# Two lent SBUF places of each layer of the second block hold first halves of split weights, in place of weights as they land

## Chip, cores and metric

The kernel runs on one core of a Trainium2 chip. The metric is the device time of one execution in microseconds (us). On this core TensorE (PE) multiplies, ScalarE (ACT) and VectorE (DVE) do elementwise work, GpSimd (POOL) helps them, and SyncE (SP) issues the transfers from HBM.

## What is computed

Two transformer blocks run one after the other on 256 tokens of width 2048, all in fp32. The first block is done when the change begins to matter. The second block has two layers, and each does this:

```python
mod = silu(c) @ w_mod[l] + b_mod[l]                      # shift, scale, gate
h = rmsnorm(x, norm_gain[l]) * (1 + scale) + shift
q_a, k_a, v_a, g_a, q_i, k_i, w_i, q_b, k_b, v_b, g_b = split(h @ w_in[l])
att = sparse_attention(norm(q_a), norm(k_a), v_a, q_i, k_i, w_i, ...)   # top 64 keys of each row
y_a = att * silu(g_a)
ret = retention(rotary(q_b), rotary(k_b) * 128 ** -0.5, v_b)
y_b = head_groupnorm(ret) * silu(g_b)
x = x + gate * (concat(y_a, y_b) @ w_out[l])
```

## The kernel before

**Weights.** All weights are read once from HBM, 512 KB at a time. Such a piece of 128 partitions x 1024 fp32 numbers is called a chunk, and the chunks are numbered in the order of their use. The first layer of the second block (layer 0) has chunks 617 to 815, layer 1 has 816 to 998. The fp32 product is formed from rounded halves (type fp32r), so each chunk of a product goes through four steps, each on an engine of its own:

- `send(j)` on SP: the transfer into a *raw place*;
- `split(j)` on ACT (its copy is recorded as L1370): the chunk, rounded, goes into a *place for first halves*, w;
- `split(j)` on DVE (recorded as L1821, SCALAR_TENSOR_TENSOR): what the first half lacks is written over the raw place, which is then called ring_r or AR_r;
- `gemm_part(j)` on PE (L150): 16 products of 128x256, eight with either half, some 1.9 us for most chunks.

Chunks of `w_mod` need only a raw place and one DVE instruction (`macc<-ring,sm,macc`). Both places of a chunk are given back when PE has finished `gemm_part(j)` (or DVE the `w_mod` chunk).

**Places.** `ring` has R1 = 7 raw places, `w1` has R2 = 5 places for first halves (printed w). While a stretch of the working buffer AR isn't used, it is lent as further places by `lend(name, base, word, kind, until, after)`: kind "raw" adds a raw place, kind "w1" a place for first halves. A lent place for first halves is printed AR_r when ACT writes it. In the second block QB and KB name the space of the rotated q and k of the retention; QI is the space of the indexer's q. `lend_start` runs at the start of a layer; `lend_qi` adds two raw places once the indexer's products are done.

**Order.** One list, `steps`, is written by a planner when the program is built, and each engine executes its own part of it, strictly in that order. The planner has no costs: it goes through the chunks, and before each `gemm` it puts a split for every chunk that has been sent and for which a place for first halves is left (`look_ahead`), and after each `gemm` a send for every raw place that has come free (`send_all`). The jobs of attention and retention (copies out of PSUM, top-k, softmax) are `phase` steps between them. So the number of places of a kind decides how far ahead of its product a chunk is sent or split, and thus between which other work its instructions stand.

Of the kernel before, what the change touches and what calls it, by code (L numbers as in the profile page):

```python
# [209 lines left out]
def program(nc, t, out, ctx):  # L210
    def sb(name, shape, dt=F32):
        return ctx.enter_context(nc.sbuf_tensor(name, shape, dt))
# [18 lines left out]
    w1 = sb("w1", [128, R2, CH], F32R)  # L231
# [156 lines left out]
    def add(w, c0, n, kt, orient, x, kind, at, need=None, dup=False, fresh=False, k0=0, quiet=False):  # L388
        b = dict(quiet=quiet, w=w, c0=c0, n=n, kt=kt, orient=orient, x=x, kind=kind, at=at, need=need, dup=dup, fresh=fresh, k0=k0)
        blocks.append(b)  # L390
        per = min(kt, CH // n)
        for k in range(0, kt, per):
            chunks.append(("w", b, k, min(per, kt - k)))
        return b
# [44 lines left out]
    def inline(kind, *at):  # L439
        job = Job(kind, *at)  # L440
        for seg in range(len(PAUSES.get(kind, ())) + 1):
            phase(job, seg)

    def enqueue(q, jobs, seg=0):

        q.append([[(j, s, (PAUSES[j.kind] + (0,))[s]) for j in jobs
                   for s in range(seg, len(PAUSES[j.kind]) + (j is jobs[-1]))], 0])
# [77 lines left out]
    def lend(name, base, word, kind, until, after):  # L525

        last = max(i for i, c in enumerate(chunks) if c[1] is until)
        plain, rounded = base
        if kind == "raw":
            s = Slot((plain[:, word:word + CH], rounded[:, word:word + CH]), in_lent[len(loans)], last)  # L530
            raw_free.append((s, after))
        else:
            s = Slot(rounded[:, word:word + CH], None, last)
            w1_free.append((s, after))
        loans[name] = s
        send_all()
# [7 lines left out]
    def norm(meanwhile=()):  # L544
        for line in xlines:
            while line[0]:
                phase(*line[0].pop(0)[:2])
        xlines.clear()
        job = Job("norm", norm_now[0])
        for seg in range(10):  # L550
            phase(job, seg)
            if 2 * seg - 2 in meanwhile:
                ensure(meanwhile[2 * seg - 2])
        norm_now[0] += 1
# [99 lines left out]
    def launch(*jobs):  # L654
        return lambda: [enqueue(queue, [j]) for j in jobs]
# [11 lines left out]
    def lend_ar(name, word, kind, until, *after):  # L667
        lend(name, (AR, ARR), word, kind, until, list(after))
# [58 lines left out]
    def layer2(L):  # L727
        WIN, h = t["w_in_2"][L], f"h{2 + L}"

        def start():  # L730
            inline("rstd", 2 + L)
            if L == 0:
                inline("decay")
                free_stages.append((NSTG, []))
            norm()
            inline("gate", L)
            if L == 0:
                enqueue(short, [Job("scalex")])

        def lend_start():  # L740
            before = (gemm, (b_out if L else b_down)["end"])
            if L == 0:
                lend_ar("W0", 11008, "raw", b_qi[0], before)
                lend_ar("V0", 8960, "raw", b_vb[0], before)
                lend_ar("V1", 9984, "w1", b_vb[0], before)
            lend_ar(f"QB0{L}", 4864, "raw", b_rot[L][0], before)
            lend_ar(f"QB1{L}", 5888, "w1", b_rot[L][1], before)
            lend_ar(f"KB0{L}", 6912, "raw", b_rot[L][2], before)
            lend_ar(f"KB1{L}", 7936, "raw", b_rot[L][3], before)

        def lend_qi():
            over = (idx_pe, ("p7", L))
            lend_ar(f"QI0{L}", 2816, "raw", b_rot[L][1], over)
            lend_ar(f"QI1{L}", 3840, "raw", b_rot[L][3], over)

        def lend_sparse():
            over = (sp_pe, ("pv", L, 3))
            lend_ar(f"W{L + 1}", 11008, "raw", b_last if L else b_qi[1], over)
            if L == 1:
                lend_ar("B0", 13312, "raw", b_last, over)  # L760
                lend_ar("B1", 14336, "raw", b_last, over)
                lend_ar("B2", 15360, "w1", b_last, over)

        def lend_retain():
            over = (ret_pe, ("sv", L, 3))
            lend_ar(f"V{2 * L + 2}", 8960, "raw", b_last if L else b_vb[1], over)
            lend_ar(f"V{2 * L + 3}", 9984, "w1", b_last if L else b_vb[1], over)

        add(WIN, 2304, 512, KT, "CM", h, "qi", (L, 0), [lend_start, start], fresh=True)
        add(WIN, 3328, 128, KT, "CM", h, "ki", (L,), dup=True)  # L770
        add(WIN, 3392, 16, KT, "TM", h, "wi", (L,))
        b_qi.append(add(WIN, 2816, 512, KT, "CM", h, "qi", (L, 1)))
        add(WIN, 1024, 128, KT, "CM", h, "kn", (L,), [launch(Job("indexer", L))])
        add(WIN, 0, 512, KT, "CM", h, "qn", (L, 0))
        add(WIN, 512, 512, KT, "CM", h, "qn", (L, 1))
        add(WIN, 1152, 128, KT, "TM", h, "va", (L,))
        for blk in range(2):
            b = add(WIN, 3408 + 512 * blk, 512, KT, "CM", h, "rot", (L, "q", blk),
                [launch(Job("retain", L, 0), Job("retain", L, 1))] if blk
                else [lend_qi, lambda: enqueue(queue, [Job("sparse", L, hp) for hp in range(4)])])  # L780
            b_rot[L][blk] = b
            b_rot[L][2 + blk] = add(WIN, 4432 + 512 * blk, 512, KT, "CM", h, "rot", (L, "k", blk))
            b = add(WIN, 5456 + 512 * blk, 512, KT, "TM", h, "vb", (L, blk))
            if blk == 0:
                b_vb.append(b)
        for blk in range(2):
            b = add(WIN, 1280 + 512 * blk, 512, KT, "CM", h, "glu", (L, "a", blk),
                    [lend_sparse] if blk else [launch(Job("retain", L, 2), Job("retain", L, 3))])
            b_g.setdefault(L, b)
        for blk in range(2):  # L790
            add(WIN, 6480 + 512 * blk, 512, KT, "CM", h, "glu", (L, "b", blk), None if blk else [lend_retain])
        for blk in range(4):
            b = add(t["w_out_2"][L], 512 * blk, 512, KT, "TM", f"o{L}", "oevac", (L, blk),
                    [lambda: inline("ahead")] if blk == 3 and L == 0 else None, fresh=blk == 0,
                    quiet=blk == 3 and L == 0)
        return b

    marks, b_g, b_qi, b_rot, b_vb = {}, {}, [], [{}, {}], []
# [1765 lines left out]
```

How the kernel before makes its waits and increments, by code:

```python
    def hold(e, J, *names):  # L841
        for name in names:
            for s, ev in J.hold[name]:
                e.wait_ge(*s.after(*ev))
# [45 lines left out]
    def given_back(e, *names):  # L891
        for name in names:
            for j in loans[name].users[-1:]:
                s, ev = over(j)
                e.wait_ge(*s.after(*ev))
# [48 lines left out]
        def send(j):  # L945
            kind, b, k, m = chunks[j]
            n, landed = b["n"], slot[j].landed
            dst = slot[j].at[0][:, 0:m * n].rearrange("p (k n) -> p k n", n=n)
            k += b["k0"]
            src = b["w"][128 * k:128 * (k + m), :].rearrange("(k p) n -> p k n", p=128)
            c0 = b["c0"]
            for s, ev in held[j]:
                e.wait_ge(*s.after(*ev))
            if b["dup"]:
                h = n // 2
                e.dma_start(dst[:, :, 0:h], src[:, :, c0:c0 + h]).then_inc(*landed.step("half", j))
                e.dma_start(dst[:, :, h:n], src[:, :, c0:c0 + h]).then_inc(*landed.step("w", j))
            else:
                e.dma_start(dst, src[:, :, c0:c0 + n]).then_inc(*landed.step("w", j))
# [1 line left out]
        def final(J, seg):  # L961
            e.wait_ge(*normed(1))
            e.wait_ge(*bias_act.after("e11"))
            e.wait_ge(*rope2_dve.after("sin"))
            e.wait_ge(*rope2_act.after("cos"))
            e.dma_start(GB, t["final_norm"].partition_broadcast(128)).then_inc(*in_final.step("row"))
# [1 line left out]
        def decay_mask(J, seg):  # L968
            e.wait_ge(*bias_act.after("e11"))
            e.wait_ge(*rope2_dve.after("sin"))
```

## Time and profile before

| | |
|---|---|
| runs | 2089.18, 2092.43, 2105.43 us; median 2092.43 |
| profiled execution | 2096.29 us |
| its span, first to last instruction | 2094.5 us |
| mean granted TensorE clock | 0.942 |
| layer 0's stretch in which the plans differ | 1278 to 1512 us |
| layer 1's stretch in which the plans differ | 1693 to 1913 us |
| HBM read | 532.55 MB, 255 GB/s over the span |

PE has the largest busy share of the engines. In a row of the profile, L150 is the matmul line, L1370 and L1821 are the lines of the helpers through which most ACT and DVE work is recorded, so one goes by the names of the tiles. A time in brackets is idle time of the engine just ahead of the instruction, with the releaser that ended it.

### The profile page before, as it was taken

What the parts mean: (1) busy time and instruction counts of PE and PEld (TensorE: products, weight loads), DVE (VectorE), ACT (ScalarE), POOL (GpSimd) and SP (SyncE); (2) the same over time, 40 slices, a digit from 0 to 9 for tenths busy, and PEclk for the clock granted to TensorE, in tenths of its full rate; (3) what the DMA queues carried; (4) which work ended last, traced back from release to release, by engine and by line L of the source; (5) the groups of instructions that cost most, each with busy time, mean ns of one, the idle gap of its engine ahead of it and who ended that gap; (6) DMA issues with size and microseconds to landing.
All of it is one profiled execution on the core that took longest, in us unless ns stands there. A gap on an engine that the chain in (4) does not pass through costs nothing. (4 is left out here: it accounts for less than half of the span.)

```text
span 2094.5 us, 34021 instructions
## 1 busy us (share of the span) xinstructions
PE 1921.8 (92%) x13292; PEld 1788.7 (85%) x13292; DVE 1711.1 (82%) x2198; ACT 1240.4 (59%) x1921; POOL 270.4 (13%) x182
## 2 busy tenths in 40 slices
PE   5998899899999997999899987999989879999798
PEld 5787889899998897989889976998878669988797
DVE  6777777875998898988898986789879876887787
ACT  5456644645566765556666658446666574566664
POOL 0000040031010012221100100132101002221020
PEclk8998899899999998999999998899999988999999
DMA  7785565865999777689889976868689867686885
GB/s 233 236 284 181 191 191 182 293 201 183 353 354 357 238 255 240 227 297 297 296 293 334 317 263 195 268 187 267 223 280 316 307 201 245 203 272 198 282 309 203
DMA packets 270764, 536.88 MB, mean 256 GB/s; under 512 B 31880, under 2 KB 40973, under 8 KB 269581
## 3 DMA queue, kind: packets, MB, share of 16 engines
q1 hardware_dynamic: 270317, 532.62, 75.9%
q8 instruction: 105, 1.72, 0.3%
q10 hardware_dynamic: 288, 2.10, 0.3%
q14 instruction: 54, 0.44, 0.1%
HBM read 532.55 MB, written 2.10 MB: 255 GB/s over the span
## 5 line engine op out<-in xcount | busy, mean ns | idle before, releaser
L150 PE MATMUL ps<-hh_r,w 128*128 128x256 f32 x3384 | 866.8, 295 | 43.6 <-DVE ring_r L1821 23.0
L150 PEld LDWEIGHTS ps<-hh_r,w 128*128 128x128 f32 x3384 | 674.2, 199 | 57.5 <-DVE ring_r L1821 27.7
L150 PE MATMUL ps<-hlo,ring_r 128*128 128x256 f32 x2816 | 707.8, 290 | 0.0
L1821 DVE SCALAR_TENSOR_TENSOR ring_r<-ring,w 128x1024 fp32r<-128x1024 f32 x449 | 555.7, 1254 | 165.0 <-ACT w L1370 162.3
L1370 ACT ACTIVATE w<-ring 128x1024 fp32r<-128x1024 f32 x449 | 465.2, 1052 | 209.8 <-DMA ring<-in_w_in 94.0
L150 PEld LDWEIGHTS ps<-hlo,ring_r 128*128 128x128 f32 x2816 | 561.4, 199 | 1.0 <-issue 0.7
L150 PE MATMUL ps<-hlo,AR_r 128*128 128x256 f32 x1104 | 268.0, 283 | 0.0
L1821 DVE SCALAR_TENSOR_TENSOR AR_r<-AR,w 128x1024 fp32r<-128x1024 f32 x172 | 214.5, 1262 | 46.0 <-ACT w L1370 45.1
L150 PE MATMUL ps<-w,AR_r 128*128 128x512 f32 x584 | 233.7, 400 | 8.7 <-DVE AR_r L1821 7.9
L1370 ACT ACTIVATE w<-AR 128x1024 fp32r<-128x1024 f32 x172 | 178.9, 1056 | 66.6 <-DMA AR<-in_w_in 23.4
L150 PEld LDWEIGHTS ps<-hlo,AR_r 128*128 128x128 f32 x1104 | 213.0, 193 | 0.3 <-issue 0.2
L150 PE MATMUL ps<-ring_r,AR_r 128*128 128x512 f32 x504 | 200.3, 397 | 0.0
L150 PE MATMUL ps<-AR 128*128 128x64 f32 (+5 forms) x1340 | 181.7, 297 | 18.7 <-DVE AR L1817 12.7
L150 PEld LDWEIGHTS ps<-AR 128*128 128x128 f32 (+1 forms) x1340 | 165.9, 197 | 28.3 <-issue 18.3
L150 PE MATMUL ps<-hh_r,AR_r 128*128 128x256 f32 x664 | 162.9, 284 | 3.1 <-DVE ring_r L1821 3.1
L150 PE MATMUL ps<-AR_r 128*128 128x512 f32 (+1 forms) x480 | 161.5, 377 | 3.1 <-DVE ring_r L1821 3.1
L1821 DVE SCALAR_TENSOR_TENSOR macc<-ring,sm,macc 128x1024 f32<-128x1024 f32 x121 | 163.4, 1350 | 0.0
L150 PEld LDWEIGHTS ps<-w,AR_r 128*128 128x128 f32 x584 | 111.4, 191 | 35.0 <-DVE AR_r L1821 5.9
L1821 DVE SCALAR_TENSOR_TENSOR ring_r<-ring,AR_r 128x1024 fp32r<-128x1024 f32 x91 | 118.6, 1308 | 20.2 <-ACT AR_r L1370 19.7
L150 PE MATMUL ps<-w,hh_r 128*128 128x512 f32 (+2 forms) x368 | 130.2, 363 | 5.4 <-DVE ring_r L1821 3.3
L150 PEld LDWEIGHTS ps<-hh_r,AR_r 128*128 128x128 f32 x664 | 127.1, 191 | 5.9 <-DVE ring_r L1821 4.9
L2407 POOL TENSOR_TENSOR AR<-AR 128x1024 int32<-128x1024 int32 (+2 forms) x25 | 55.2, 2209 | 549.8 <-DVE AR L1821 439.1
(204 smaller groups left out, 2765.5 us busy)
## 6 DMA issues: line engine op xcount, KB each, us to landing
ring<-in_w_in SPq DMA_DIRECT2D x285, 512.0 KB, 5.2
ring<-in_w_mod SPq DMA_DIRECT2D x131, 512.0 KB, 5.5
ring<-in_w_up SPq DMA_DIRECT2D x115, 512.0 KB, 5.5
AR<-in_w_in SPq DMA_DIRECT2D x83, 512.0 KB, 5.7
ring<-in_w_out SPq DMA_DIRECT2D x63, 512.0 KB, 6.5
ring<-in_w_down SPq DMA_DIRECT2D x63, 512.0 KB, 5.9
AR<-in_w_up SPq DMA_DIRECT2D x61, 512.0 KB, 5.5
AR<-in_w_mod SPq DMA_DIRECT2D x48, 512.0 KB, 6.1
```

Source lines behind the costliest of these rows:

```text
L150: return e.matmul(o, l, x, start=start, stop=stop, skip_group_check=True)
L1370: return e.activation(o, i, ACT.Copy, scale=scale)
L1821: return e.scalar_tensor_tensor(o, a, s, b, op0, op1)
L2407: return e.tensor_tensor(o, a, b, op)
```

## The change

In each layer, the two places KB0 and KB1 are lent for first halves and no longer for weights as they land. Chunks are sent, split and multiplied in the same order as before, by the same instructions; the places they use differ, and the point in each engine's program at which a send or a split stands.

```diff
             lend_ar(f"QB0{L}", 4864, "raw", b_rot[L][0], before)
             lend_ar(f"QB1{L}", 5888, "w1", b_rot[L][1], before)
-            lend_ar(f"KB0{L}", 6912, "raw", b_rot[L][2], before)
-            lend_ar(f"KB1{L}", 7936, "raw", b_rot[L][3], before)
+            lend_ar(f"KB0{L}", 6912, "w1", b_rot[L][2], before)
+            lend_ar(f"KB1{L}", 7936, "w1", b_rot[L][3], before)
```

Worked out from the planner, in layer 0 (layer 1 is alike): where there were 11 raw places and 7 for first halves, there are now 9 and 9, until `lend_qi` adds two raw places ahead of chunk 662. When PE begins a `gemm` in chunks 640 to 661, the chunks sent beyond it were 10 and are now 8; those split, with its own, were 7 or 8 and are now up to 9, which is all that has been sent. From chunk 664 on, 9 are sent ahead where there were 11, and 7 to 8 split as before. The plans are the same again from about chunk 715 and, in layer 1, about 914.

First place: ACT in layer 0, around the copies of the first half of q_a out of PSUM (L1376 and L1370 with VT). The names in_ring and in_lent are the signals of landing. Before:

```order
L1370 ACTIVATE w<-ring 128x1024 [waits gemm_done,in_ring5]
L1370 ACTIVATE AR_r<-ring 128x1024 [waits gemm_done,in_ring6]
L1370 ACTIVATE AR_r<-ring 128x1024 [waits gemm_done,in_ring0]
L1376 ACTIVATE stg<-ps 128x512 [waits gemm_done,idx_pool]
L1370 ACTIVATE AR<-ps,VT 128x512
L1376 ACTIVATE stg<-ps 128x512 [waits gemm_done,idx_pool]
L1370 ACTIVATE AR<-ps,VT 128x512
L1370 ACTIVATE w<-ring 128x1024 [waits gemm_done,in_ring1]
```

The same place after the change:

```order
L1370 ACTIVATE AR_r<-ring 128x1024 [waits gemm_done,in_ring4]
L1370 ACTIVATE AR_r<-ring 128x1024 [waits gemm_done,in_ring5]
L1370 ACTIVATE w<-ring 128x1024 [waits gemm_done,in_ring6]
L1376 ACTIVATE stg<-ps 128x512 [waits gemm_done,idx_pool]
L1370 ACTIVATE AR<-ps,VT 128x512
L1376 ACTIVATE stg<-ps 128x512 [waits gemm_done,idx_pool]
L1370 ACTIVATE AR<-ps,VT 128x512
L1370 ACTIVATE w<-ring 128x1024 [waits gemm_done,in_ring0]
```

The split just ahead of the four copies was that of chunk 657, which SP sent behind the product of chunk 646; it is now that of chunk 659, sent behind the product of chunk 650, the last but one ahead of the copies.

Second place: DVE in layer 0, around the first product of the retention (`stg<-ps,AR`, L1813), whose masked scores PE takes next. Before:

```order
L1821 SCALAR_TENSOR_TENSOR macc<-ring,sm,macc 128x1024 [waits mod_dve,in_ring5]
L1821 SCALAR_TENSOR_TENSOR ring_r<-ring,w 128x1024 [waits w1_done]
L1994 RECIPROCAL sm<-sm 128x4 [waits sp_act]
L1821 SCALAR_TENSOR_TENSOR ring_r<-ring,AR_r 128x1024 [waits w1_done]
L1813 TENSOR_TENSOR stg<-ps,AR 128x512 [waits ret_pe,in_decay,rot_pool,qn_dve]
L1813 TENSOR_TENSOR stg<-ps,AR 128x256
```

The same place after the change:

```order
L1821 SCALAR_TENSOR_TENSOR macc<-ring,sm,macc 128x1024 [waits mod_dve,in_ring1]
L1821 SCALAR_TENSOR_TENSOR AR_r<-AR,AR_r 128x1024 [waits w1_done]
L1994 RECIPROCAL sm<-sm 128x4 [waits sp_act]
L1821 SCALAR_TENSOR_TENSOR AR_r<-AR,AR_r 128x1024 [waits w1_done]
L1821 SCALAR_TENSOR_TENSOR ring_r<-ring,w 128x1024 [waits w1_done]
L1813 TENSOR_TENSOR stg<-ps,AR 128x512 [waits ret_pe,in_decay,rot_pool,qn_dve]
L1813 TENSOR_TENSOR stg<-ps,AR 128x256
```

One more split, which waits for ACT's, stands between the reciprocal and the product.

Third place: ACT in layer 0, ahead of the copies of the second half of the retention's q (`stg<-ps 64x512`). Before:

```order
L1376 ACT_TABLE_LOAD
L1376 ACTIVATE sm<-sm 128x4 [waits ret_act]
L1370 ACTIVATE w<-ring 128x1024 [waits gemm_done,in_ring6]
L1370 ACTIVATE stg<-ps 64x512 [waits gemm_done,rot_pool]
L1370 ACTIVATE stg<-ps 64x512
```

The same place after the change:

```order
L1376 ACT_TABLE_LOAD
L1376 ACTIVATE sm<-sm 128x4 [waits ret_act]
L1370 ACTIVATE AR_r<-ring 128x1024 [waits gemm_done,in_ring2]
L1370 ACTIVATE w<-ring 128x1024 [waits gemm_done,in_ring3]
L1370 ACTIVATE stg<-ps 64x512 [waits gemm_done,rot_pool]
L1370 ACTIVATE stg<-ps 64x512
```

Two splits, of chunks 710 and 711, stand ahead of the copies in place of one, of chunk 710; chunk 711 is now sent behind the product of chunk 702, two products ahead of the copies.

## Rows read from the trace of the kernel before

**Rows 1.** The page, busy time of each engine over the span

```profile
PE 1921.8 (92%) x13292; PEld 1788.7 (85%) x13292; DVE 1711.1 (82%) x2198; ACT 1240.4 (59%) x1921; POOL 270.4 (13%) x182
```

**Rows 2.** The page, groups: splits (busy, mean ns of one, idle before, releaser)

```profile
L1821 DVE SCALAR_TENSOR_TENSOR ring_r<-ring,w 128x1024 fp32r<-128x1024 f32 x449 | 555.7, 1254 | 165.0 <-ACT w L1370 162.3
L1370 ACT ACTIVATE w<-ring 128x1024 fp32r<-128x1024 f32 x449 | 465.2, 1052 | 209.8 <-DMA ring<-in_w_in 94.0
```

**Rows 3.** Windows: length; busy PE, PEld, DVE, ACT, POOL; clock, DMA share, GB/s

```profile
1303.00:1345.00 42.00, 40.59 (x288) 40.59 (x289) 32.81 (x35) 21.26 (x26) 0.00 (x0) 0.80 0.83 269
...
1426.00:1465.00 39.00, 36.07 (x231) 32.29 (x230) 36.06 (x37) 22.47 (x37) 15.59 (x8) 1.00 0.81 265
...
1512.00:1560.00 48.00, 43.68 (x290) 39.15 (x290) 36.74 (x41) 27.49 (x67) 3.91 (x2) 1.00 0.85 277
...
1888.00:1893.00 5.00, 5.00 (x25) 5.00 (x25) 3.31 (x4) 2.08 (x9) 0.00 (x0) 0.50 0.00 0
```

**Rows 4.** PE's waits, 1304 to 1426 (total us, times, longest)

```profile
PE ps L150 <- DVE ring_r L1821: 7.8, 1, 7.8
PE ps L150 <- DVE AR_r L1821: 0.3, 1, 0.3
```

**Rows 5.** PE's waits, 1426 to 1512

```profile
PE ps L150 <- DVE stg L1813: 2.1, 1, 2.1
PE ps L150 <- issue: 1.8, 1, 1.8
...
PE ps L150 <- ACT stg L1370: 1.1, 1, 1.1
```

**Rows 6.** PE's waits in layer 1, 1718 to 1840, then 1840 to 1915

```profile
PE ps L150 <- ACT AR L1370: 1.5, 1, 1.5
...
PE ps L150 <- DVE stg L1813: 4.6, 1, 4.6
```

**Rows 7.** ACT's longest wait, 1345 to 1396, then 1512 to 1560

```profile
ACT w L1370 <- PE ps L150: 13.9, 10, 2.3
...
ACT w L1370 <- DMA ring<-in_w_in: 14.6, 9, 3.0
```

**Rows 8.** Issues, 1345 to 1396, then 1404 to 1426 (median us to landing last)

```profile
ring<-in_w_in SPq DMA_DIRECT2D x14, 512.0 KB, 4.0
...
ring<-in_w_in SPq DMA_DIRECT2D x5, 512.0 KB, 4.8
```

**Rows 9.** Timeline, SP, ACT and PE, first half of q_a (start, us)

```profile
1373.11 0.37 SPq L959 DMA_DIRECT2D AR<-in_w_in  x1
...
1375.04 0.60 ACT L1376 ACTIVATE stg<-ps 128x512 f32<-128x512 f32 x1 [0.81 <-PE ps L150]
...
1376.69 1.84 PE L150 MATMUL ps<-cst,stg 128*128 128x1 f32 x16
```

**Rows 10.** Timeline, SP, ACT and PE, around the first q_b copies

```profile
1420.92 0.37 SPq L959 DMA_DIRECT2D ring<-in_w_in  x1
...
1423.17 2.42 ACT L1370 ACTIVATE stg<-ps 64x512 f32<-64x512 f32 x4
1425.62 0.87 ACT L1370 ACTIVATE AR<-ps 128x512 f32<-128x512 f32 x2
...
1427.75 1.47 PE L150 MATMUL ps<-AR 128*128 128x256 f32 x8
```

**Rows 11.** Timeline, DVE, the last split and the retention's product behind it

```profile
1473.39 1.23 DVE L1821 SCALAR_TENSOR_TENSOR ring_r<-ring,AR_r 128x1024 fp32r<-128x1024 f32 x1 [2.59 <-ACT AR_r L1370]
1474.54 1.01 DVE L1813 TENSOR_TENSOR stg<-ps,AR 128x512 f32<-128x512 f32 x2
```

**Rows 12.** Timeline, SP, ACT and PE, around the second q_b copies

```profile
1489.06 0.37 SPq L959 DMA_DIRECT2D ring<-in_w_in  x1
...
1492.33 2.42 ACT L1370 ACTIVATE stg<-ps 64x512 f32<-64x512 f32 x4 [1.09 <-PE ps L150]
...
1499.27 0.63 PE L1341 MATMUL ps<-cst,stg 128*128 128x128 f32 x4 [1.32 <-DVE stg L1813]
```

**Rows 13.** Timeline, DVE, one of the splits between steps of top-k

```profile
1387.51 1.23 DVE L1821 SCALAR_TENSOR_TENSOR AR_r<-AR,w 128x1024 fp32r<-128x1024 f32 x1
```

## The prediction

> **What bounds the kernel now.** First the busy shares of the page. PE is busy for 1921.8 of 2094.5 us, DVE for 82% and ACT for 59% [rows 1]; so an ACT or DVE instruction costs time only where it makes PE wait, and one that is late by more than its slack costs the rest in full. The change adds no instruction, no byte and no matmul. All it can do is shift when a chunk is sent and where its splits stand, so I read next how the weights are supplied in the stretches in which the plans differ.
>
> The windows come second [rows 3]. In 1303 to 1345 PE is busy for 40.59 of 42 us at 0.80 clock; in 1426 to 1465 DVE (36.06 of 39) is as full as PE (36.07); in 1512 to 1560, where the lent places are gone and both plans have 7 raw and 5 first-half places, PE still gets 43.68 of 48 us. The reader is to see that DMA isn't full in any of them (0.81 to 0.85). Transfers take 4.0 us from issue to landing, 4.8 in a fuller stretch [rows 8], against 1.9 us of PE for a chunk: eight chunks ahead would be some 15 us, so the number of raw places isn't short in itself.
>
> Third come PE's own waits. In layer 0 up to 1426 they are one of 7.8 us at the layer's start and one of 0.3 us for a weight [rows 4]; then 2.1, 1.8 and 1.1 us, none for a weight [rows 5]. In layer 1 they are 1.5 us behind an ACT copy and 4.6 us behind DVE's retention product [rows 6]. **Weights that are split too late cost PE almost nothing now.** More places for first halves can win little here.
>
> Fourth come ACT's waits. In 1345 to 1396 ACT waits at its splits for PE to free a first-half place (13.9 us in 10 waits, no wait for a transfer); in 1512 to 1560, with 7 and 5 places, it waits for transfers (14.6 us in 9) [rows 7]. With 9 and 9 places the first stretch takes on the second's nature: every chunk sent is split at once, so ACT, which executes in order, stands at a split until that chunk has landed, and the copies out of PSUM behind it are late.
>
> A rule of the Trainium skill speaks against the change. The trace shows the ACT splits of 1345 to 1396 waiting for no transfer [rows 7]. The Trainium skill, "DMA: Bandwidth & Descriptors", section "Rules for kernel authors", says to issue a transfer early and wait for its semaphore late, and the change does the reverse for ACT's splits. The rule names no size; by it the time rises, and by the rows alone the question is what stands behind each split.
>
> **The change, part by part.** Instructions: zero, the same splits of 1.05 us on ACT and 1.25 on DVE [rows 2]. The four places where the order changes for a copy that PE soon needs are these, in layer 0:
>
> *A, first half of q_a.* The split ahead of the copies is now that of chunk 659, sent when PE has done chunk 650: 1373.11 [rows 9], where before this slot sent chunk 661. Landing takes 4.0 [rows 8], the split 1.05 [rows 2]: 1378.2. The copies began at 1375.04 [rows 9], so they start 3.1 us later. PE's sums on them ran at 1376.69 [rows 9], just as the second copy ended, with no slack. Term: +3.1.
>
> *A2, the second half of q_a.* The same order, but both top-k and softmax work stand between and give slack. No row shows how much: bounds 0 and 3.1 (A). I take 0.5, near zero, because PE goes through five chunks without a wait there and needs the sums late.
>
> *B, first half of q_b.* The split of chunk 678 stands at the same step as before, but its chunk is sent at 1420.92 [rows 10] and no longer two products earlier. It lands at 1420.9 + 4.8 = 1425.7 [rows 8], is split at 1426.8, then come the copies of 2.42 and 0.87 [rows 10]: 1430.0. PE's products of attention (ps<-AR) ran at 1427.75 [rows 10]. Term: 1430.0 - 1427.75 = +2.2.
>
> *C, the retention's first product.* DVE waited 2.59 us for an ACT split, split, then started the product at 1474.54 [rows 11], and this product is what PE's wait of 2.1 us ends on [rows 5]. Now one more ACT split stands ahead of the ACT copies and one more between them and the product. Term: 2 x 1.05 - 0.1 overlap = +2.0 at least; a landing on top would make it 2.6. I take 2.0. Every microsecond shows, as PE waits there already.
>
> *D, second half of q_b.* The split of chunk 711 now stands ahead of the copies. It is sent behind chunk 702 at 1489.06 [rows 12], after chunk 710 (0.4 for its issue), lands 4.2 later (between 4.0 and 4.8) [rows 8] and is split by 1494.8. The copies began at 1492.33 [rows 12]: 2.5 late. DVE's rotation and the retention's group norm queue behind them, and PE already waits 1.32 for that at 1499.27 [rows 12]. Term: +2.5.
>
> Layer 0: 3.1 + 0.5 + 2.2 + 2.0 + 2.5 = 10.3. **Layer 1** has the same A, A2 and B. At C only one ACT split is added (1.05, and up to a half more with its landing; I take 1.4), at D PE's slack is some 0.6 larger (1.9). Near its end the place of one chunk (918) comes back with chunk 911's product instead of 909's, when only some 2 to 3 us of slack are left: bounds 0 and one landing of 4.8 [rows 8], I take 1.5, a third, since the DVE queue has slack of its own. Sum: 3.1 + 0.5 + 2.2 + 1.4 + 1.9 + 1.5 = 10.6. Gross: 20.9.
>
> *What is absorbed.* A, A2 and B stop PE for 5.8 us in a layer before a stretch that DVE bounds (36.06 of 39 busy) [rows 3]. There PE has waits that don't grow if it comes late: 2.1 + 1.8 + 1.1 = 5.0 in layer 0 [rows 5], and the 4.6 and a like 1.8 in layer 1 [rows 6]. Bounds: nothing, or 5.0 and 5.8. DVE is nearly full, but part of its work hangs on PE's products, so I take somewhat less than the upper: 4 and 5, together -9.
>
> *What is gained.* Between steps of top-k DVE takes one split in about 3.5 us (one of them at 1387.51) [rows 13], slower than PE's 1.9, and only 0.3 us of PE wait comes of it [rows 4]; with 9 chunks split ahead that wait goes: -0.3 a layer. The 1.5 us of layer 1 [rows 6] come from a copy behind a split that waits for its landing; the order there is changed, and I take -1.4 (bounds -1.5 and 0, and the reverse can't be excluded by the rows). The waits of 7.8 and 4.6 us at the layers' starts end on a split that stands behind the norm in either plan: 0. Together -2.
>
> *Covers.* Two fewer sent ahead: at chunks 640 to 661 there are 8, some 15 us of PE work, against 4.0 to 4.8 of landing plus 1.05 and 1.25 of splits, 7.1 at most. That covers the smaller number of raw places wherever ACT is not held up. If the cover fails, PE waits for weights: see the rivals.
>
> Sum: 20.9 - 9 - 2 = +9.9. The span becomes 2104.4 and the profiled execution 2106.2 (it lies 1.8 above its span). The profiled run was 3.9 above the median, so I carry the difference and not the level: 2092.4 + 9.9 = 2102.3.
>
> The landings come from the trace. By the Trainium skill, "DMA: Bandwidth & Descriptors", section "Anatomy of one DMA", a transfer costs about 2.0 us and its bytes by 436 GB/s, for 512 KB an estimate of 3.2 us, measured there on another issue path. The trace has 4.0 to 4.8. By this figure A, B and D would be smaller by 0.8 to 1.6 each, and the sum by some 6, which still leaves it above zero.
>
> **The rivals.** *Absorbed.* All that A, B, C and D hold up is small against the slack of later work, or PE's waits at C and D merely take another name. For it: DVE and PE are equally full in the middle [rows 3], and each wait is under 3.1. Against it: C and D lie on waits of PE itself [rows 5, 12]. Upper absorption (10.8) with C and D halved (20.9 - 4 - 10.8 - 2) gives +4; with both covered wholly, 0. Time: 2092 to 2096, say 2094.
>
> *Deeper splits win.* A chunk that is split nine ahead is ready however long top-k holds DVE, and fewer transfers are in flight at once. Then the waits of 0.3, 1.5 and a part of 7.8 and 4.6 [rows 4, 6] go. At most 14.2 us hang on weights in these rows; I count the small ones and a fifth of the large: -1.8 - 2.5 = -4, so 2088. Against it: the large ones start with the norm, not with a place.
>
> *Starved.* The raw places are what matters: chunks after the layer's start land later because their place comes back later, while the window 1303 to 1345 has PE at 40.59 of 42 [rows 3], and PE waits once or twice for a landing of 4 to 5 us in each layer. +4 to +8 in place of, or beside, the terms above: 2100.
>
> *Slower by over 1%.* This is the other side of the bound. Its mechanism is PE's clock. After the 4.6 us wait in layer 1 the granted clock was 0.50 (1.2 GHz) for the 5 us from 1888 on [rows 3], which costs 2.5 us. PE's short waits (2.1, 1.8, 1.1) [rows 5] left the window 1426 to 1465 at 1.00. If the new waits at A, B, C and D, alone or joined, become long enough to lower the clock in both layers, each costs some 2.5 more: 8 x 2.5 = 20 over the 20.9 - 9 - 2 gives +30, 2122. It decides once A, B and D are 4 us and more, where I have 2.2 to 3.1.
>
> *The change doesn't do what it says.* The order shows that it does: behind the product of chunk 650 SP sends chunk 661 before and chunk 659 after, and so on through chunks 641 to 659.
>
> **How the numbers follow.** A measurement of this kernel tells about 1%, 21 us, from no change. Chances: the forecast (+5 to +16) 0.42; absorbed (-4 to +5) 0.27; starved (+2 to +20) 0.12; deeper splits win (-4 and below, to -10) 0.11; slower by over 1% 0.08. The predicted time is 2102. The range goes from 2087, which leaves out half of the deeper splits' case, to 2116: the gross 20.9 with C at 2.6 in both layers and little absorbed (20.9 + 1.8 + 1 = 23.7). Outside lie the clock's case and the tails. Faster by over 1%: 0.02; within 1%: 0.90; slower: 0.08.
>
> **What would show it.** In the profile after: between 1345 and 1396 ACT waits for DMA where it waited for PE; PE waits 2 to 3 us at the sums behind the first half of q_a, about 2 at the first attention products, and 3 to 4.5 at the retention's first product; top-k costs no PE wait. Total PE busy time unchanged but for clock. Wrong would be: PE waits named ring_r or AR_r in these stretches (starved), PE's waits summing to what they were (absorbed), or landing times that fall, since fewer transfers are in flight, and take A, B and D with them.

## The result, and the profile after

The kernel after the change takes 2131.22 us (median of 4 runs, 2130.18 to 2133.71), the kernel before 2094.76 us beside it (4 runs). The ratio is 1.0182, 95% interval 1.0146 to 1.0218: slower by some 38 us (the medians differ by 36.5, the two profiled executions by 37.4). The profiled execution took 2133.71 us, its span is 2131.9 us. The forecast was 2102 us with 2116 as the upper end.

Where it went is read from windows that hold the same work in both traces. The first pair runs from the end of chunk 641's product to the end of chunk 717's (columns as in [rows 3]). The kernel before:

```profile
1347.15:1516.61 169.46, 162.27 (x1195) 151.82 (x1195) 143.54 (x226) 101.69 (x184) 45.27 (x30) 0.96 0.72 227
```

The kernel after the change, the same 1195 matmuls, then a window at A, and then the four stretches at half clock (granted clock 0.50, 1.2 GHz) that the kernel before doesn't have, or has shorter. They lie behind A, A2, the second attention product and D, the places that the prediction names and the table below measures:

```profile
1344.85:1533.69 188.84, 170.25 (x1195) 159.18 (x1195) 147.14 (x225) 101.70 (x175) 45.78 (x29) 0.92 0.66 210
1376.00:1381.00 5.00, 2.91 (x18) 2.73 (x17) 3.17 (x10) 4.18 (x7) 2.85 (x2) 0.79 0.76 206
1378.90:1385.80 6.90, 6.90 (x34) 6.90 (x34) 6.63 (x29) 2.40 (x3) 0.24 (x1) 0.51 0.16 45
1402.80:1416.50 13.70, 13.66 (x63) 13.42 (x63) 3.22 (x3) 2.51 (x5) 0.00 (x0) 0.50 0.29 96
1464.30:1467.70 3.40, 3.40 (x11) 2.74 (x11) 3.40 (x3) 1.93 (x3) 3.40 (x3) 0.50 0.42 157
1515.50:1518.90 3.40, 3.40 (x18) 3.40 (x17) 2.74 (x4) 1.79 (x5) 0.00 (x0) 0.50 0.00 0
```

The kernel before, its only two stretches at half clock in this part (A2, and behind the wait at C, where the kernel after the change has 3.4 us too):

```profile
1398.30:1408.50 10.20, 10.20 (x49) 10.11 (x48) 5.59 (x5) 2.42 (x6) 0.00 (x0) 0.50 0.32 100
1476.80:1480.20 3.40, 3.40 (x18) 3.40 (x18) 3.40 (x5) 2.09 (x9) 0.00 (x0) 0.50 0.01 3
```

The reader is to see two parts of the loss. The stretch is 188.84 - 169.46 = 19.4 us longer. PE's idle time grew from 7.2 to 18.6 us, by 11.4; its busy time for the same matmuls grew from 162.3 to 170.3, by 8.0, because the granted clock fell from 0.96 to 0.92, in pieces at 0.50 (1.2 GHz): 30.8 us of them where there were 13.6, and half of the 17.2 more is 8.6. Layer 1 is alike: from the end of chunk 840's product to that of 924's it is 183.83 us before (1762.01 to 1945.84) and 204.46 after (1780.10 to 1984.56), 20.6 longer, PE busy for 174.45 and 181.68. The first block differs by 2.3 us and the rest by less, so the two stretches hold the loss.

PE's waits after the change, 1343 to 1434, answer to [rows 4]:

```profile
PE ps L150 <- ACT AR L1370: 3.8, 2, 2.1
PE ps L150 <- DVE AR L1818: 0.8, 1, 0.8
PE ps L150 <- DVE stg L1818: 0.8, 1, 0.8
```

and those in 1434 to 1530 to [rows 5]:

```profile
PE ps L1341 <- DVE stg L1813: 4.6, 1, 4.6
PE ps L150 <- issue: 4.2, 2, 2.3
PE ps L150 <- DVE stg L1813: 3.8, 1, 3.8
PE ps L150 <- ACT stg L1370: 0.7, 1, 0.7
```

No wait is put down to a split weight (ring_r, AR_r); those with a name are for the layer's other work, and the two without one (issue) stand ahead of products of the attention, the first, of 2.3 us, at B. ACT's waits in 1345 to 1396 answer to the first row of [rows 7]:

```profile
ACT w L1370 <- DMA AR<-in_w_in: 12.2, 4, 6.7
ACT AR_r L1370 <- DMA ring<-in_w_in: 10.9, 8, 3.1
ACT w L1370 <- DMA ring<-in_w_in: 3.8, 4, 1.9
```

ACT waited for PE at its splits before; now it waits for transfers, as forecast. How that reaches PE shows at A, the first half of q_a, in the timeline of SP, ACT and PE (answers to [rows 9]):

```profile
1372.48 0.37 SPq L959 DMA_DIRECT2D ring<-in_w_in  x1
...
1376.12 1.06 ACT L1370 ACTIVATE w<-ring 128x1024 fp32r<-128x1024 f32 x1 [1.88 <-DMA ring<-in_w_in]
1377.08 0.58 ACT L1376 ACTIVATE stg<-ps 128x512 f32<-128x512 f32 x1
...
1378.38 3.04 PE L150 MATMUL ps<-cst,stg 128*128 128x1 f32 x16 [2.09 <-ACT AR L1370]
1381.28 0.56 PE L150 MATMUL ps<-hh_r,w 128*128 128x256 f32 x1
```

Chunk 659 is issued at 1372.48, has landed at 1376.1, is split, and only then come the copies and PE's sums, after 2.09 us of wait. What the forecast didn't have is behind it: the sums take 3.04 us where they took 1.84 [rows 9], and the clock is at half from 1378.9 to 1385.8. The place cost 5.3 us, of which 2.1 are wait.

The table has the loss of each place against the kernel before, from the ends of the same chunks' products in the two profiled executions (layer 0 / layer 1). A row of an experiment is read the same way. How good a single profile is shows in layer 1 of e4_layer0_only, which has the plan of the kernel before: 0.1 us in all places but A2, where it is off by 1.7.

| us | indexer | A | A2 | B | 2nd attention product | C | D |
|---|---|---|---|---|---|---|---|
| forecast | 0 / 0 | 3.1 / 3.1 | 0.5 / 0.5 | 2.2 / 2.2 | less than 0 | 2.0 / 1.4 | 2.5 / 1.9 |
| after | 1.7 / 2.7 | 5.3 / 5.4 | 2.9 / 2.7 | 2.4 / 2.4 | 1.2 / 0.1 | 1.0 / 0.2 | 4.9 / 5.7 |
| e1_kb_none | 0 / 0 | 0 / 0 | 0.7 / 6.2 | 2.2 / 2.6 | -0.5 / -0.1 | 1.5 / -1.1 | 2.5 / 0 |
| e8_lag1 | 0.4 / 1.3 | -0.1 / -0.1 | -0.7 / -0.6 | 0.5 / -0.2 | -1.9 / 1.7 | -0.5 / 1.5 | 3.0 / 0.1 |
| e9_lag1_early | 0.4 / 1.5 | -0.1 / -0.1 | 1.0 / 3.8 | 2.2 / 2.3 | -0.4 / 0.7 | 2.3 / 0.2 | 4.8 / 5.8 |
| e10_lag1_late | 1.6 / 2.6 | 3.8 / 5.2 | -0.7 / 1.1 | 0.4 / -0.2 | -2.0 / 0.8 | -0.2 / 1.2 | 1.3 / 0 |
| e5_filler | 1.5 / 1.9 | 3.9 / 2.5 | -0.4 / -1.9 | 2.1 / 2.5 | -0.4 / 0.1 | 2.6 / -1.0 | 5.2 / 6.4 |
| e6_quiet | 1.3 / 3.4 | -0.1 / -0.1 | -2.3 / -0.4 | 0.3 / -0.2 | 1.4 / 1.0 | 3.9 / 1.7 | 5.3 / 3.5 |

**D** isn't what the forecast made of it. The lines around it, SP, DVE, ACT and PE, after the change (answers to [rows 11, 12]):

```profile
1487.88 2.43 PE L150 MATMUL ps<-AR,stg 128*128 128x128 f32 x11 [3.77 <-DVE stg L1813]
...
1492.98 0.37 SPq L959 DMA_DIRECT2D ring<-in_w_in  x1
...
1498.06 2.52 DVE L1821 SCALAR_TENSOR_TENSOR ring_r<-ring,w 128x1024 fp32r<-128x1024 f32 x2 [4.97 <-ACT w L1370]
1500.50 0.70 DVE L1817 TENSOR_SCALAR sm<-sm 128x4 f32<-128x4 f32 x1
...
1502.98 0.31 ACT L1376 ACTIVATE stg<-stg 128x128 f32<-128x128 f32 x1 [3.66 <-DVE stg L1813]
...
1506.26 1.04 ACT L1370 ACTIVATE AR_r<-ring 128x1024 fp32r<-128x1024 f32 x1
1507.21 1.04 ACT L1370 ACTIVATE w<-ring 128x1024 fp32r<-128x1024 f32 x1
1508.28 2.42 ACT L1370 ACTIVATE stg<-ps 64x512 f32<-64x512 f32 x4
...
1514.83 0.63 PE L1341 MATMUL ps<-cst,stg 128*128 128x128 f32 x4 [4.59 <-DVE stg L1813]
```

PE waits 3.77 us at C. The sends of chunks 707 and 708 stand behind chunk 698's product, which comes after that wait, so SP issues them at 1492.98 only. Both are split at once: DVE stands for 4.97 us at them, and the retention's mean (sm<-sm at 1500.50), the first link of its group norm, is behind both in DVE's queue. ACT waits 3.66 us for the step behind the mean, so its splits of 710 and 711 and the copies behind them come late, though neither split waits for a landing (711's is the one more of this place, 1.0 us). DVE takes the same two splits and the rotation of the copies before the norm's last step, and that step is what PE waits 4.59 us for at 1514.83; 3.4 us at half clock follow. In the kernel before, 707 is sent ahead of that wait and 708 is split behind the mean.

### The profile page after: what moved, and what is told of

Read it like the earlier page. It is cut to its first block and busy times, and to the rows that moved or that the text cites. A ratio compares the mean times of both kernels' runs of the same rounds, so it can differ in the third digit from the quotient of the medians.

```text
span 2131.9 us, 34021 instructions
## 1 busy us (share of the span) xinstructions
PE 1929.6 (91%) x13292; PEld 1793.6 (84%) x13292; DVE 1717.8 (81%) x2198; ACT 1242.0 (58%) x1921; POOL 270.1 (13%) x182
## 5 line engine op out<-in xcount | busy, mean ns | idle before, releaser
L150 PE MATMUL ps<-hh_r,w 128*128 128x256 f32 x3208 | 822.9, 295 | 47.5 <-DVE ring_r L1821 26.3
L150 PE MATMUL ps<-hlo,ring_r 128*128 128x256 f32 x2912 | 731.6, 290 | 0.0
L150 PEld LDWEIGHTS ps<-hh_r,w 128*128 128x128 f32 x3208 | 639.9, 199 | 60.7 <-DVE ring_r L1821 32.3
L1370 ACT ACTIVATE w<-ring 128x1024 fp32r<-128x1024 f32 x444 | 459.2, 1052 | 231.1 <-DMA ring<-in_w_in 142.1
L150 PEld LDWEIGHTS ps<-hlo,ring_r 128*128 128x128 f32 x2912 | 580.2, 199 | 1.0 <-issue 0.7
L150 PE MATMUL ps<-hlo,AR_r 128*128 128x256 f32 x1008 | 244.5, 283 | 0.0
L150 PE MATMUL ps<-hh_r,AR_r 128*128 128x256 f32 x840 | 206.5, 285 | 3.1 <-DVE ring_r L1821 3.1
L1370 ACT ACTIVATE w<-AR 128x1024 fp32r<-128x1024 f32 x155 | 161.4, 1056 | 77.1 <-DMA AR<-in_w_in 42.5
L150 PEld LDWEIGHTS ps<-hlo,AR_r 128*128 128x128 f32 x1008 | 194.2, 193 | 0.3 <-issue 0.2
L1821 DVE SCALAR_TENSOR_TENSOR macc<-ring,sm,macc 128x1024 f32<-128x1024 f32 x128 | 172.6, 1349 | 10.2 <-DMA ring<-in_w_mod 10.2
L1821 DVE SCALAR_TENSOR_TENSOR ring_r<-ring,AR_r 128x1024 fp32r<-128x1024 f32 x110 | 140.2, 1279 | 41.6 <-ACT AR_r L1370 39.9
L150 PEld LDWEIGHTS ps<-hh_r,AR_r 128*128 128x128 f32 x840 | 161.5, 192 | 6.5 <-DVE ring_r L1821 3.8
L1370 ACT ACTIVATE AR_r<-ring 128x1024 fp32r<-128x1024 f32 x110 | 115.6, 1053 | 65.4 <-DMA ring<-in_w_in 44.6
```

The lines of the kernel that those rows point to most:

```text
L150: return e.matmul(o, l, x, start=start, stop=stop, skip_group_check=True)
L1370: return e.activation(o, i, ACT.Copy, scale=scale)
L1821: return e.scalar_tensor_tensor(o, a, s, b, op0, op1)
```

## Experiments

Each was timed beside the kernel before on its chip (15 to 19 runs of it, medians 2092.4 to 2093.5 us).

**e1_kb_none: as few raw places, no more first halves.** Against the kernel after the change (a second line, which skips the names that are lent for nothing, is left out here):

```diff
-            lend_ar(f"KB0{L}", 6912, "w1", b_rot[L][2], before)
-            lend_ar(f"KB1{L}", 7936, "w1", b_rot[L][3], before)
```

> KB0 and KB1 are lent for nothing in both layers: 9 raw places and 7 for first halves, as few raw places as after the change and as few for first halves as before. The split just ahead of the copies of the first half of q_a is of chunk 657, sent behind chunk 648, three products ahead of the copies (after the change 659, one product ahead; before 657, five ahead). Theory 'late copies' (what costs is that ACT stands at a split until a chunk sent just before has landed, and the copies behind it are late): ACT waits at most 1 us for landings there, PE's wait at those sums is gone; the second q_b place keeps part of its wait, since chunk 710 is sent as late as after. 2094 to 2106 us, ratio 1.000 to 1.006. Rival 'too few raw places' (weights are late because they are sent later): all of the loss stays, 2125 to 2135 us.

Measured: 2104.65 us, ratio 1.0070 (1.0044 to 1.0095), +12 us. ACT's waits in 1345 to 1375 (its page numbers the copy L1368):

```profile
ACT w L1368 <- PE ps L150: 9.3, 5, 2.3
ACT AR_r L1368 <- PE ps L150: 3.8, 2, 1.9
...
ACT w L1368 <- DMA ring<-in_w_in: 0.6, 2, 0.3
```

ACT waits for PE again, and A costs nothing in either layer. Two thirds of the loss have gone although two raw places fewer are there than before. B stays at 2.2 and 2.6 us, as it should: its chunk 678 is sent as late as after the change, and is split at the same step. So a late send costs where a split follows it at once, and the deep splitting made every split such a one. In the profile what stays is B (4.8 us in both layers), C and D of layer 0 (4.0) and, in layer 1, 6.2 us at A2, where PE waited 1.3 us for a weight (ring_r) and then ran at half clock; layer 0 lost 0.7 in the same order. The profiled execution took 2111.38 us, 6.7 above the median, so the 6.2 aren't typical, but a small part of this loss is weights that come late.

**e2_kb0_only: one place each.**

```diff
-            lend_ar(f"KB1{L}", 7936, "w1", b_rot[L][3], before)
+            lend_ar(f"KB1{L}", 7936, "raw", b_rot[L][3], before)
```

> Only KB0 goes to first halves, KB1 stays a raw place: 10 raw, 8 for first halves. Last splits ahead of copies: chunk 658 sent three products ahead (q_a), chunk 678 sent three ahead (q_b), and 710 four ahead (second q_b). 'Late copies': landing of some 4 us has passed within three products of 1.9 to 2.9 us, so nearly nothing: 2092 to 2102 us. 'Too few raw places': about half of the loss, 2110 to 2116 us.

Measured: 2103.84 us, ratio 1.0055 (1.0032 to 1.0078), +11 us: above the 2102 of one theory, far below the 2110 of the other. In its profile A and D are within 0.1 us of the kernel before in both layers and B within 0.8; what it loses (7.5 us in all) lies at the layers' starts, 4.2 and 3.4 us, ahead of the places. There a late copy shows again, in ACT's timeline, layer 0:

```profile
1319.64 1.06 ACT L1370 ACTIVATE AR_r<-ring 128x1024 fp32r<-128x1024 f32 x1 [3.42 <-DMA ring<-in_w_in]
1320.60 1.07 ACT L1370 ACTIVATE AR<-ps 128x512 f32<-128x512 f32 x2
```

PE waits 3.5 us for this copy, and 3.3 us for its like in layer 1; the kernel before made it at 1317.42, and PE waited 0 and 1.5 us. It is the same cause at a place that I hadn't listed.

**e3_lag2 and e8_lag1: the places of the change, fresh chunks not split.** In `next_split`, against the kernel after the change (1 in place of 2 for e8_lag1):

```diff
-        return j if w1_free and j < at_send[0] else None
+        late = 2 if j < len(chunks) and chunks[j][1]["x"] in ("h2", "h3") else 0
+        return j if w1_free and j < at_send[0] - late else None
```

> The kernel after the change with 9 raw and 9 first-half places, but in the second block's input projections the planner splits no chunk that is among the last two sent. Sends stand exactly where they stand after the change; only the splits stand later. 'Late copies': PE's waits behind ACT copies go, 2092 to 2102 us. 'Too few raw places': nothing changes, 2128 to 2135 us.

> As e3_lag2, but only the chunk sent last is held back from being split: at q_a the split ahead of the copies is of chunk 658, sent two products ahead (after the change one, in e3_lag2 three). 'Late copies' makes it a matter of degree: landing of 3.7 plus split 1.05 against two products of 1.9 to 2.9 us, so at most 1 us late at A and no half clock; a rest at B and D. 2098 to 2108 us, above e3_lag2 and far below after.

Measured: 2100.29 us, ratio 1.0034 (1.0021 to 1.0046), with two held back; 2095.67 us, 1.0006 (0.9992 to 1.0020), with one. Sends, raw places and first-half places are those of the kernel after the change, and only the splits stand one chunk later. Of the 40.1 us that the change cost in its two stretches, 34 come back (6.0 stay, most in layer 1); another 5.8 us come from between chunks 717 and 816, where both kernels have the same places and only the held-back split is different (e11_lagall_before gains 6.9 us there). So too few raw places can't be what costs the bulk; some 6 us are left to it or to something else. I had expected less of e8_lag1 than of e3_lag2, and it was the other way round; with two held back DVE gets its splits late enough that PE waits for weights (1.2 us in 1343 to 1434, 4.6 us in three waits behind), and A2 costs 4.1 and 5.9 us. ACT's waits of e8_lag1 in 1345 to 1375:

```profile
ACT AR_r L1371 <- DMA ring<-in_w_in: 9.4, 7, 2.5
ACT w L1371 <- DMA AR<-in_w_in: 3.7, 3, 1.7
ACT w L1371 <- DMA ring<-in_w_in: 1.9, 2, 1.6
```

ACT still waits 15.0 us for transfers (15.2 after the change), and A costs nothing. **The waits for landings cost nothing by themselves here; the last one ahead of a copy does,** and with one more product of time it is over before the copy is due.

**e4_layer0_only.**

```diff
-            lend_ar(f"KB0{L}", 6912, "w1", b_rot[L][2], before)
-            lend_ar(f"KB1{L}", 7936, "w1", b_rot[L][3], before)
+            lend_ar(f"KB0{L}", 6912, "raw" if L else "w1", b_rot[L][2], before)
+            lend_ar(f"KB1{L}", 7936, "raw" if L else "w1", b_rot[L][3], before)
```

> The change in layer 0 alone. If the two layers' losses are separate, about half: the trace of after lost some 19 us in chunks 640 to 717 and some 20 in 838 to 920, so 2111 to 2116 us, and layer 1's chunks take the time that they took before. If there were one common cause (where a place lies, a slower chip), the loss would not follow the layer.

Measured: 2110.89 us, ratio 1.0084 (1.0069 to 1.0099), +18 us, half of the whole. Layer 1's A, B, C and D are within 0.1 us of the kernel before, its A2 within 1.7.

**e5_filler: PE kept busy ahead of the q_a sums.** In PE's `qn`, against the kernel after the change:

```diff
                 hold(e, J, "b")
+                for u in range(0 if J.at[1] % 2 else 16):
+                    fp(pb(J, "b")[:, 0:256], hhi[:, 0, 0:128], hhi[:, 0, :])
                 e.wait_ge(*qn_act.after("copy", *J.at))
```

> The kernel after the change, with 16 products of 128x256 that nobody reads, on PE ahead of its wait for the q_a copies, twice in a layer (A and A2); they are overwritten by the sums. In the trace of after PE waits 2.1 us at A in layer 0 and then runs at 1.2 GHz to 1385.7. Theory 'the wait lowers the clock' (half of the loss at A is clock): PE isn't idle there, the clock stays at 2.4 GHz behind A, and 2 to 3 us come back at each A, some less at A2: 2120 to 2127 us. Rival 'the clock falls by itself there' (the sums with one column each): 16 products of 0.12 us are covered by the wait or add to it, 2131 to 2136 us.

Measured: 2126.61 us (2123.18 to 2130.34; a fourth run, of 3078.99 us at a mean clock of 0.551, which I can't explain, is left out), ratio 1.0162 (1.0140 to 1.0185) against the 1.0182 of the change: the intervals overlap, so the total alone decides nothing. The place does, in PE's timeline:

```profile
1378.75 2.08 PE L150 MATMUL ps<-hh_r 128*128 128x256 f32 x16
1380.89 2.18 PE L150 MATMUL ps<-cst,stg 128*128 128x1 f32 x16
```

and in the windows in front of and behind it:

```profile
1378.00:1382.00 4.00, 3.88 (x32) 3.60 (x30) 2.37 (x5) 3.29 (x6) 2.68 (x2) 1.00 0.92 251
1382.00:1388.00 6.00, 5.95 (x38) 5.99 (x39) 5.77 (x24) 1.91 (x2) 0.19 (x1) 0.72 0.16 34
```

The filler takes the wait's place, the sums are back to 2.18 us, and the clock stays at 1.00 until 1382; but it falls behind, to 0.72 over 6 us, which is 3.4 us at half where there were 6.9. A costs 3.9 and 2.5 us where it cost 5.3 and 5.4, A2 -0.4 and -1.9 where it cost 2.9 and 2.7. So at A 1.4 and 2.9 us were clock that the wait had taken (A2's larger gain, 3.3 and 4.6, may hold other clock: the kernel before runs at 1.2 GHz for a while there too). The sizes are rough: the four gains sum to 12 us in this execution, the fastest of the three, while the medians differ by 4.6. Why the clock still falls behind the filled wait stays open.

**e6_quiet: no split ahead of a block's last product.**

```diff
-            if not (b["quiet"] and k0 + m == b["kt"]):
+            if not ((b["quiet"] or b["kind"] in ("qn", "rot")) and k0 + m == b["kt"]):
```

> The kernel after the change, but no split is put ahead of the last product of a block of q_a, q_b or k_b, so the copies of those blocks stand behind the split of one chunk less: at q_a 658, sent two products ahead of the copies, and at the second q_b 708, sent six ahead. Sends are unchanged. 'Late copies': the waits at A, A2, B and D shrink by most of a product's time, 1.9 us, and the half clock behind A goes: 2100 to 2112 us. If the loss lay with weights or raw places: 2128 us and more.

Measured: 2113.44 us, ratio 1.0099 (1.0075 to 1.0124), +20 us where some 38 stood. A, A2 and B are gone, D isn't (5.3 and 3.5), and C is larger (3.9 and 1.7), as I read it because the splits left out ahead of a block's end are made up for there. That refuted my cause for D: chunk 711's split no longer stands ahead of the copies there. The splits of 707 and 708 still stand ahead of the retention's mean, which pointed to the chain shown above.

**e7_qb1_raw: a step the other way, from the kernel before.**

```diff
-            lend_ar(f"QB1{L}", 5888, "w1", b_rot[L][1], before)
+            lend_ar(f"QB1{L}", 5888, "raw", b_rot[L][1], before)
```

> The kernel before, with QB1 too as a raw place in both layers: 12 raw and 6 for first halves, a step in the other direction. Chunks are sent earlier and split one later. 'Late copies': ACT waits for no landing there before either, so nothing to win, and one split less ahead of top-k may cost a wait for weights: 2090 to 2100 us. 'Too few raw places': faster than before, 2075 to 2088 us.

Measured: 2099.58 us, ratio 1.0023 (1.0002 to 1.0045). More raw places don't help. The step also takes a place for first halves, and the profile shows 1.9 us of PE waits for late splits (ring_r) in 1343 to 1434, so this speaks less plainly than e8_lag1.

**e9_lag1_early and e10_lag1_late: e8_lag1 in two parts.** The condition of e8_lag1 with one more term, for e9_lag1_early:

```diff
+        late = 1 if j < len(chunks) and chunks[j][1]["x"] in ("h2", "h3") and chunks[j][1]["kind"] in ("qi", "ki", "wi", "kn", "qn", "va") else 0
```

and with `("rot", "vb", "glu")` for e10_lag1_late.

> The kernel after the change; the chunk sent last is held back from being split only for the blocks from qi to va, so the splits ahead of the indexer's work and of the first q_a copies stand later, and all from the chunks of the first q_b block on stand as after the change. In the traces of before and after the places lose in us: indexer 1.7 and 2.7 (layer 0, layer 1), A 5.3 and 5.4, A2 2.9 and 2.7, B 2.4 and 2.4, second attention product 1.2 and 0.1, C 1.0 and 0.2, D 4.9 and 5.7. If the places are independent, the indexer and A come back, 15 us: 2114 to 2119 us. If each wait only moves work onto the next one (the losses are one chain), less than 8 come back: above 2122.

> The same for the blocks from the first q_b block on alone, which moves the splits at A2 (whose last splits are of q_b chunks), B, C and D. In particular the split of chunk 708 stands behind the retention's mean step on DVE again, where after the change it stood ahead of it and DVE waited 5.0 us for the splits of 707 and 708, which SP had sent only after PE's wait at C. Independent places: 25 us come back, 2103 to 2109 us, A stays with its 5 us in each layer and D goes. One chain: whatever A starts is carried on, 2115 and more.

Measured: 2117.81 us, ratio 1.0115 (1.0081 to 1.0149), and 2112.48 us, 1.0087 (1.0057 to 1.0117). Against 1.0182 they give back 0.67% and 0.95%, 14 and 20 us, together 34 of the 37 that e8_lag1 gives back (1.0182 - 1.0006). Some 3 us of e10_lag1_late's share come from behind chunk 717, as in e8_lag1. The places are nearly independent: without the wait at A, D stays at 4.8 and 5.8; with it, D falls to 1.3 and 0. The first time lies in the range that independence had given (2114 to 2119), the second 3 us above it (2103 to 2109) and below that of one chain (2115). DVE around the mean in e10_lag1_late, where the split of 708 is behind it (its page numbers the lines one higher):

```profile
1485.51 2.46 DVE L1822 SCALAR_TENSOR_TENSOR ring_r<-ring,w 128x1024 fp32r<-128x1024 f32 x2
...
1491.41 1.22 DVE L1822 SCALAR_TENSOR_TENSOR ring_r<-ring,w 128x1024 fp32r<-128x1024 f32 x1 [2.24 <-ACT w L1371]
```

One split and 2.24 us of wait stand in front of the mean where there were two and 4.97, and PE's wait at the transposes fell from 4.6 to 2.6 us.

**e11_lagall_before and e12_lagall_after.** The chunk sent last is never split, in the whole program; e11 with the places of before, e12 with those of after:

```diff
-        return j if w1_free and j < at_send[0] else None
+        late = 1 if at_send[0] < len(chunks) else 0
+        return j if w1_free and j < at_send[0] - late else None
```

> The kernel before, with the chunk sent last never split, in both blocks. If ACT's standing at a split until the landing costs elsewhere too (7 raw and 5 first-half places leave ACT waiting for transfers in much of the program), up to 1% faster, 2075 to 2090 us. If weights come too late by one product more, slower, up to 2105 us. Likeliest: 2085 to 2097 us.

> The same with the places of the kernel after the change. Against e11 it shows what the two places are worth once the split waits for no fresh chunk: 'late copies' says that they are worth about nothing either way, the same as e11 within 6 us; if deeper splits help at all, faster than e11 by 1 to 5 us.

Measured: 2087.27 us, ratio 0.9978 (0.9962 to 0.9994), and 2093.90 us, 0.9999 (0.9981 to 1.0017). The first is the fastest kernel of the study, by some 5 us, small, but its interval lies below 1; in its profile 7 us come from layer 0's part behind chunk 717. With the split rule mended, the two places as first halves take 6.6 us more than as raw places (the expectation allowed 6); the two intervals overlap a little, so this rest is likely but not shown.

## Why the prediction was wrong

**What bounds.** Right for layer 0: PE waited 0.3 us for a weight before, and not at all after. In layer 1 the waits for ring_r are 1.6 us before (1762 to 1946) and 2.7 after (1780 to 1985), near the end, at chunk 918's place. Right too that ACT would wait for landings where it had waited for PE, 27 us in 1345 to 1396.

**A.** The mechanism was right: landing 3.6 us (4.0 taken), PE's wait 2.1 (3.1 taken). The size was not: the place cost 5.3 and 5.4, since 3.2 us of half clock followed. That is the first failed step. I had the clock as a rival, "it decides once A, B and D are 4 us and more", read off one wait of 4.6 us; it took 2.1 us here. The kernel before had shown as much. I wrote that its waits of 2.1, 1.8 and 1.1 us [rows 5] left the window 1426 to 1465 at 1.00, but the one of 2.1 us, at C, ends at 1475.65, behind that window (PE's timeline):

```profile
1475.65 1.86 PE L150 MATMUL ps<-AR,stg 128*128 128x128 f32 x12 [2.14 <-DVE stg L1813]
```

and the window behind it was at 0.68:

```profile
1475.00:1480.00 5.00, 4.35 (x25) 4.38 (x26) 5.00 (x8) 2.34 (x10) 0.00 (x0) 0.68 0.30 106
```

That reading put the clock at nothing in the sum. The wait's length alone doesn't tell, since the 1.8 us left the clock at 1.00. In layer 0 some 8 of the 19.4 us are clock, half of each stretch that is new: 3.4 at A, 1.7 at A2, 1.7 behind the second attention product and 1.7 at D.

**A2.** I took 0.5 between bounds of 0 and 3.1 for want of a row. It is 2.9 and 2.7: 1.66 us of PE wait (the split ahead of the copies waited 1.11 us for its landing) and a longer piece at 0.50, 13.7 us where there were 10.2. The slack that I assumed wasn't there; the upper bound was the place of the same kind, A, and should have been taken.

**B.** 2.2 forecast, 2.4 and 2.4 measured; e1_kb_none and e8_lag1 show it to be chunk 678's landing.

**C.** 2.0 and 1.4 forecast, 1.0 and 0.2 measured.

**D.** 2.5 and 1.9 forecast, 4.9 and 5.7 measured, by another cause: DVE's queue ahead of the retention's mean, and sends held back by PE's wait at C. Chunk 711's landing, which I had priced, cost nothing. (The lines are layer 0's; that layer 1 has the same cause is supported by e6_quiet and e10_lag1_late, where its D is 3.5 and 0, and not followed line by line.) I had read only the splits ahead of ACT's copies, and had not asked what stands behind each DVE split.

**Absorbed, -9.** The second failed step, and the largest. I let PE's lateness at A, A2 and B vanish in its waits of the second stretch [rows 5], as if those ended at a fixed time. They end on work that follows PE's own products and on chunks sent behind them, so they came later with it. In layer 0 they were 2.1 + 1.8 + 1.1 = 5.0 us and are 3.8 + 1.9 + 0.7 = 6.4 (the other "issue" wait, of 2.3 us, is B itself); in layer 1 they were 4.6 + 1.8 = 6.4 and are 4.6 + 0.9 + 0.9 = 6.4. Measured absorption: none that I can find. e9_lag1_early tests it: it takes 13.4 us away at the indexer's place and at A, and 14 come back in the total. The table's "after" row sums to 19.4 and 19.2, and with the 1.5 us of chunk 918's place in layer 1 (1.5 forecast) to 20.7.

**The indexer.** Not seen: 1.7 and 2.7 us, as two waits of 0.8 us for DVE in layer 0. DVE's steps for the indexer (L1818) are behind splits as well; e8_lag1 halves the loss or better.

**Gained, -2.** The wait of 0.3 us is gone; that of 1.5 us in layer 1 is still there (1.6 us).

Gross, I had 20.9 us; the places' measured sum is 40.1. Of the 19.2 between, A and its clock are 4.5, A2 4.6, D 6.2, the indexer 4.4, B and the second attention product 1.7, and C is 2.2 less. Then 9 were taken off that should have stayed, and 2 for gains. The upper end of the range (20.9 + 1.8 + 1 = 23.7) took nothing off and was still short, by the same places; its last term, 1, had no row behind it.

**The rivals.** "Slower by over 1%" came true by its mechanism, clock on top of waits, joined to a larger gross, at waits half as long as it had asked for. "Starved" fell as the cause of the bulk with e3_lag2 and e8_lag1; the 6 us that e8_lag1 still loses in the two stretches may be partly its own; "absorbed" and "deeper splits win" fell with the result.

## What to carry to other kernels

Where an engine runs a queue in order, what matters isn't how long it waits for transfers but which instruction stands behind the last of those waits: a look-ahead that takes a chunk as soon as it has been sent puts a landing in front of whatever comes next, and one chunk of distance cured most of it here. More buffers for the later stage of a pipeline, taken from the earlier one, shorten just this distance. (The Trainium skill, "DMA: Bandwidth & Descriptors", section "Rules for kernel authors", says to issue a transfer early and to wait for its semaphore late. The pair of 2131.22 us and e8_lag1's 2095.67 us agrees, and e8_lag1's 15.0 us of waits at no cost add that the wait need only be late for what stands behind it.) And delays of an engine whose progress triggers the sends aren't absorbed by its later waits; count them in full, with the clock behind them, until a row shows a wait that ends at a time of its own.

## What the runs showed of the hardware

A PE wait of 2.1 us at A, with sums of one column behind it, was followed by 6.9 us at 1.2 GHz (1378.9 to 1385.8), and the wait of 2.1 us at C of the kernel before by 3.4 us (1476.8 to 1480.2), while waits of 1.8 us (the kernel before, up to 1453.89) and of 2.3 us (after the change, up to 1437.86) left the clock at 1.00. It also fell without any wait: in the kernel before PE was busy for all 8 us from 1396 to 1404, its sums of one column among them, and the clock was at 0.64 there. Filling the wait at A with 16 products kept the clock up through the wait, but it fell afterwards for part of 1382 to 1388 (0.72). What sets this off was not settled.

The fewer chunks in flight did not land faster to speak of. The median of the issues in 1343 to 1434 is, for the kernel after the change, over 22 transfers:

```profile
ring<-in_w_in SPq DMA_DIRECT2D x22, 512.0 KB, 4.3
```

and for the kernel before, over 19:

```profile
ring<-in_w_in SPq DMA_DIRECT2D x19, 512.0 KB, 4.3
```
